# Attention's operands in a one-core hybrid SSD and attention block: queries stored as they are used, keys read with a doubled source, blank columns dropped

## The chip, the cores and the metric

One core of one Trainium2 chip. The metric is the device time of one execution in microseconds. All numbers below are of this kernel, which runs one whole layer in one program: projections, SSD scan, attention, merge, routed experts, output norm.

## The reference, cut to what matters

The layer has SEQ = 1024 latent and CTX = 256 context tokens, D_MODEL = 1024, 16 query heads and 4 key and value heads of 64. One input projection gives, among others, q, k and v. Latent q and k are rotated. A block of 128 latent queries reads all 256 context keys and the latent keys of three blocks, its own and its neighbours:

```python
kp = jnp.pad(k, ((0, 0), (WINDOW, WINDOW), (0, 0), (0, 0)))
vp = jnp.pad(v, ((0, 0), (WINDOW, WINDOW), (0, 0), (0, 0)))
def block(i):
    start = i * ATTN_BLOCK
    qb = lax.dynamic_slice_in_dim(qg, start, ATTN_BLOCK, axis=1)
    kb = lax.dynamic_slice_in_dim(kp, start, span, axis=1)
    ...
    s_loc = jnp.where(valid, s_loc, -jnp.inf)
    s_ctx = jnp.einsum("bqkrd,bskd->bkrqs", qb, k_ctx).astype(jnp.float32)
    p = jax.nn.softmax(jnp.concatenate([s_loc, s_ctx, s_sink], -1), axis=-1).astype(v.dtype)
```

The padded columns are masked. The output of the whole block is (1, 1024, 1024) in float32. Context queries aren't needed, as only the latent stream is put out.

## The kernel before, in words

The program is a row of stages, each one block in which every engine has its own list of instructions; engines order themselves by semaphores, and a stage's engines leave its block together. Float32 products are made of split operands: a number is kept as a high part `hi`, rounded to the type that TensorE multiplies, and the rest `lo`.

**Stage f** (`project_f_stage`) makes the outputs that have channels on partitions: x/B/C, then queries and keys (`NQK` = 10 tiles of 128 channels: 8 of queries with two heads each, 2 of keys), then gates. A tile of queries or keys is rotated, split by ScalarE (`keep_hi`, L575) and VectorE (`keep_lo`, L651) into the double-buffered tiles `qk_hi` and `qk_lo`, and stored by GpSimd (`store_split`, L710) to the DRAM tensors `qkH` and `qkL`. These have one row per channel and `KV_TOK` = 1536 columns: context, 128 blank columns, latent tokens, 128 blank columns. GpSimd fills the key rows' blanks with zeros at the stage's start (L695). ScalarE overwrites a buffer of `qk_hi` two tiles later, and waits for its store (`qk_out`, L574). After the tiles the same buffers take weights for another product.

**The states stage** stores the values token by token in `vT`, which has the same blanks (L1124, GpSimd); next GpSimd loads and scales chunks for the SSD states.

**The scan stage** (`scan_output_stage`) runs 32 units u: 8 chunks of 128 tokens times 4 groups. SyncE stores each unit's result `y` to `yT` (`store`, L1325), and behind the store it issues what `Early.load` (L1221) lists for this u: attention's first operands, into the slots of `shared` that the last chunks no longer need. Units 23, 24: the high keys, lower then upper 64 partitions. 25: query tile 0. 26: masks and identity. 27, 28: the low keys. 29: query tile 1. 30: another mask. `y` has one buffer per group, so the result of unit u is written (GpSimd's `finish`, L1533; the last unit's by VectorE, L1514) only when the store of unit u - 4 has landed. SyncE is one queue: what it issues late makes all behind it late.

**The attention stage** takes scores as two products in a row: a full one of 128 rows, `q` tile times `k1`, and one of 64 rows, times `k2` (L1674, L1678). The 128 rows of a query tile are the head's high part (64) and its low part (64), in this order for even heads and the other way round for odd ones; `k1` has the high keys twice, one copy in each half of the partitions, and `k2` the low keys twice. A query tile is 128 partitions x 16 heads x 128 queries. `load_query` (L1213) gathers it by four transfers, one for each half of the partitions and each parity of head; there are four buffers, and from tile 4 on SyncE loads tile m when tile m - 4 is scored. `load_key` (L1210) loads one half of the partitions for all four groups. Before its first score TensorE waits for both keys, the constants, and GpSimd's memset `a_ones` (L1846); VectorE waits for the sink (L1649, `a_negsink` L1807) and for all of `yT`'s stores, and each maximum (L1775) lets the next scores into the two score banks.

Of the kernel before, what the change touches and what calls it, by code (L numbers as in the profile page):

```python
# [23 lines left out]
P = 128  # L24
# [39 lines left out]
BLANK = WINDOW  # L64
KV_LAT0 = CTX + BLANK
KV_TOK = KV_LAT0 + SEQ + BLANK


def shape_constants():
# [13 lines left out]
    for b in range(LCHUNK):  # L83
# [3 lines left out]
    edges = np.stack([masks[:, :, CTX:CTX + P].transpose(0, 2, 1), masks[:, :, CTX + 2 * P:].transpose(0, 2, 1)], 2)  # L87
# [3 lines left out]
        "edges": np.ascontiguousarray(edges).reshape(LCHUNK, P, 2 * P),  # L91
# [5 lines left out]
        "flat": np.stack([np.zeros(KVH * KV_TOK, np.float32), np.ones(KVH * KV_TOK, np.float32)]),  # L97
# [225 lines left out]
def project_f_stage(s, cond_cols, mod, hi, lo, first, ahead, xbcF, xbcT, qkH, qkL, gF):  # L323
# [7 lines left out]
    with ExitStack() as st:  # L331
# [9 lines left out]
        zeros = own(st, nc, "f_zeros", [P, BLANK])  # L341
# [29 lines left out]
        zeros_made, blanks_out = s.sem("f_zeros_made"), s.sem("f_blanks_out")  # L371
# [18 lines left out]
        with nc.Block() as block:  # L390
# [297 lines left out]
            def _(pool):  # L688
                s.credit(pool, turned_out)

                pool.memset(zeros[:], 0.0).then_inc(zeros_made, 1)
                pool.wait_ge(zeros_made, 1)
                for part in (qkH, qkL):
                    for a in (CTX, KV_LAT0 + SEQ):
                        pool.dma_start(part[QH * HD:, a:a + BLANK].rearrange("(f p) t -> p f t", p=P),  # L695
                                       zeros[:].unsqueeze(1).to_broadcast([P, NQK - NQ, BLANK])).then_inc(blanks_out, 16)

# [39 lines left out]
                for b in range(2):  # L737
                    pool.wait_ge(qk_out[b], 16 * (NQK + NQK - NQ))
                    pool.wait_ge(turned_out[b], 8 * NT + 16)
# [7 lines left out]
                pool.wait_ge(blanks_out, 64)  # L747
                for b in range(2):
                    pool.wait_ge(qk_out[b], 16 * (NQK + NQK - NQ))
                    pool.wait_ge(wide_out[b], 8 * (NX - NXS))  # L750
                    pool.wait_ge(turned_out[b], 8 * NT + 16)
# [23 lines left out]
def project_states_stage(s, hi, lo, ahead, zT, vT, xbcT, tabs, cumrow, logrow, before):  # L775
# [20 lines left out]
    with ExitStack() as st:  # L796
# [4 lines left out]
        zeros = own(st, nc, "t_zeros", [P, VW])  # L801
# [25 lines left out]
        zeros_made, zeros_out = s.sem("t_zeros_made"), s.sem("t_zeros_out")  # L827
# [30 lines left out]
        with nc.Block() as block:  # L858

            @block.sync  # L860
            def _(sp):
# [5 lines left out]
                def store_v(n):  # L867
                    sp.wait_ge(acc_free, n + 1)
                    at = n * P if n < CCHUNK else KV_LAT0 + (n - CCHUNK) * P
# [237 lines left out]
            def _(pool):  # L1107
# [27 lines left out]
                pool.wait_ge(zeros_out, 32)  # L1135
# [43 lines left out]
class Early:  # L1179


    def __init__(self, s, st):
# [3 lines left out]
        NK, NQ, END = KVH * KV_TOK, QH * P, KVH * KV_TOK + QH * P  # L1186
# [34 lines left out]
    def load(self, s, eng, qkH, qkL, u):  # L1221
        low, high = slice(0, HD), slice(HD, P)
# [20 lines left out]
def scan_output_stage(s, later, early, qkH, qkL, xbcT, xbcF, zT, tabs, cumrow, logrow, before, yT):  # L1243
# [14 lines left out]
    with ExitStack() as st:  # L1258
# [39 lines left out]
        with nc.Block() as block:  # L1298

            @block.sync  # L1300
            def _(sp):
# [34 lines left out]
                for u in range(UNITS):  # L1336
                    store(u)
                    early.load(s, sp, qkH, qkL, u)
# [218 lines left out]
def attention_stage(s, later, early, yT, qkH, qkL, vT, aF):  # L1557
# [11 lines left out]
    NV = KV_TOK // P  # L1569
    STEP_COUNT = PAIRS + 4  # L1570

    def tiles(n):
        first = 1 if n == 0 else 0
        last = 2 if n == LCHUNK - 1 else 3
        return [(P * t, t) for t in range(CCHUNK)] + [(CTX + P * (t - first), CCHUNK + n + t) for t in range(first, last)]
# [1455 lines left out]
```

## Time and profile before

| what | before |
|---|---|
| runs | 2635.36, 2635.18, 2631.15 us; median 2635.18 |
| profiled execution, own time | 2638.86 us |
| its span, first to last instruction | 2637.1 us |
| TensorE busy | 2404.6 us, 91% |
| VectorE, ScalarE, GpSimd busy | 1696.2, 1140.2, 497.9 us |
| mean granted TensorE clock | 0.946 of full speed |
| DMA | 564.42 MB in 348009 packets, mean 214 GB/s |

A row of the profile names the line of the kernel, the engine, the operation, and `out<-in` by the program's names. A name with a q (SPq, POOLq) is an engine's sequencer: it issues DMAs and waits, and isn't counted as busy. "DMA share" is the mean busy share of the core's 16 DMA engines, and GB/s what they moved. "To landing" is the time from an issue to the last byte. Idle time of an engine that isn't the bottleneck costs nothing.

### The profile page before, as it was taken

How to read it: one execution, taken by the hardware profiler on the slowest of the kernel's cores; microseconds unless marked ns; L12 is line 12 of the kernel's file. 1: busy time of each engine (PE TensorE's matmuls, PEld its weight loads, DVE VectorE, ACT ScalarE, POOL GpSimd, SP SyncE). 2: the span in 40 equal slices, each digit the busy share in tenths (PEclk: the TensorE clock that was granted, in tenths of full speed). 3: DMA queues.
4: the chain of work that ended last, by engine and by line, in shares of the span. 5: the costliest groups of instructions: out<-in, count | busy, mean ns of one | idle time of the engine just before them, and what ended most of it. 6: DMA issues, size and time to landing. Idle time of an engine off the chain costs nothing. (4 is left out here: it accounts for less than half of the span.)

```text
span 2637.1 us, 34496 instructions
## 1 busy us (share of the span) xinstructions
PE 2404.6 (91%) x13468; PEld 1967.1 (75%) x13468; DVE 1696.2 (64%) x1900; ACT 1140.2 (43%) x1538; POOL 497.9 (19%) x410
## 2 busy tenths in 40 slices
PE   7899999999999997996999899998872999999992
PEld 2788888887798876664666599997762788888882
DVE  5555555544235663775666677665556899999996
ACT  3333332221123111454666644433332677777772
POOL 0000000011003440785111100001323011011112
PEclk9899999999999998988999999998975999999996
DMA  6222234776436875989331299895326899999994
GB/s 224 78 72 80 82 108 122 183 228 224 139 119 210 295 272 161 315 280 237 56 82 41 74 271 259 243 254 176 124 84 248 308 405 403 402 398 396 396 369 143
DMA packets 348009, 564.42 MB, mean 214 GB/s; under 512 B 22069, under 2 KB 257605, under 8 KB 325017
## 3 DMA queue, kind: packets, MB, share of 16 engines
q1 hardware_dynamic: 322522, 460.39, 52.3%
q0 software_dynamic: 23376, 97.36, 11.5%
q10 hardware_dynamic: 1968, 4.72, 0.5%
q8 instruction: 95, 1.56, 0.3%
q14 instruction: 48, 0.39, 0.0%
HBM read 452.74 MB, written 104.42 MB: 211 GB/s over the span
## 5 line engine op out<-in xcount | busy, mean ns | idle before, releaser
L2650 DVE TENSOR_TENSOR e_wlo<-e_w,e_whi 128x2048 fp32r<-128x2048 f32 x188 | 425.7, 2290 | 42.9 <-ACT e_whi L2599 41.6
L2599 ACT CAST e_whi<-e_w 128x2048 fp32r<-128x2048 f32 x192 | 365.4, 1910 | 124.7 <-PE e_gu L2776 83.5
L460 PE MATMUL f_lat<-h_hi,w_hi 128*128 128x512 f32 x800 | 253.9, 398 | 8.0 <-DVE w_lo L611 8.0
L460 PE MATMUL f_lat<-h_lo,w_hi 128*128 128x512 f32 x800 | 251.3, 395 | 0.0
L460 PE MATMUL f_lat<-h_hi,w_lo 128*128 128x512 f32 x800 | 251.1, 395 | 0.0
L2110 PE MATMUL b_acc<-b_hi,b_whi 128*128 128x256 f32 x768 | 218.7, 285 | 7.7 <-issue 7.7
L2110 PE MATMUL b_acc<-b_lo,b_whi 128*128 128x256 f32 x768 | 218.1, 284 | 0.0
L2110 PE MATMUL b_acc<-b_hi,b_wlo 128*128 128x256 f32 x768 | 218.1, 284 | 0.0
L611 DVE TENSOR_TENSOR w_lo<-w_raw,w_hi 128x1024 fp32r<-128x1024 f32 x50 | 61.2, 1226 | 171.6 <-ACT w_hi L530 171.6
L460 PEld LDWEIGHTS f_lat<-h_hi,w_hi 128*128 128x128 f32 x800 | 137.9, 189 | 38.3 <-DVE w_lo L611 8.6
L460 PEld LDWEIGHTS f_lat<-h_lo,w_hi 128*128 128x128 f32 x800 | 140.1, 188 | 29.9
L460 PEld LDWEIGHTS f_lat<-h_hi,w_lo 128*128 128x128 f32 x800 | 140.0, 188 | 29.8
L2110 PEld LDWEIGHTS b_acc<-b_hi,b_whi 128*128 128x128 f32 x768 | 148.3, 193 | 8.1 <-issue 8.1
L2110 PEld LDWEIGHTS b_acc<-b_lo,b_whi 128*128 128x128 f32 x768 | 148.2, 193 | 0.0
L2110 PEld LDWEIGHTS b_acc<-b_hi,b_wlo 128*128 128x128 f32 x768 | 148.2, 193 | 0.0
L625 DVE SCALAR_TENSOR_TENSOR conv_acc<-conv_in,conv_tap_cols,conv_acc 128x1284 f32<-128x1284 f32 (+1 forms) x96 | 145.0, 1511 | 3.4
L2776 PE MATMUL e_gu<-e_whi,e_xhi 128*128 128x512 f32 x512 | 140.3, 396 | 3.7 <-DVE e_xlo L2654 2.4
L2776 PE MATMUL e_gu<-e_wlo,e_xhi 128*128 128x512 f32 x512 | 138.7, 393 | 0.0
L2776 PE MATMUL e_gu<-e_whi,e_xlo 128*128 128x512 f32 x512 | 138.0, 392 | 0.0
L2845 POOL DMA_INDIRECT moe<-e_y,e_token x15 | 42.2, 2811 | 498.3 <-DVE e_y L2671 468.0
L1775 DVE CUSTOM_DVE_ANT_0 a_rows<-a_a_ps,shared 128x640 f32<-128x640 f32 (+1 forms) x128 | 96.0, 788 | 48.2 <-PE a_a_ps L1678 47.6
L1729 ACT ACTIVATE a_rows<-a_rows,a_negtop 128x640 f32<-128x640 f32 (+1 forms) x128 | 101.6, 796 | 31.1 <-DVE a_negtop L1781 31.0
(373 smaller groups left out, 5355.4 us busy)
## 6 DMA issues: line engine op xcount, KB each, us to landing
e_w<-in_w_gate_up SPq DMA_DIRECT2D x128, 1024.0 KB, 10.8
e_w<-in_w_down SPq DMA_DIRECT2D x64, 1024.0 KB, 9.0
w_raw<-in_w_in SPq DMA_DIRECT2D x50, 512.0 KB, 3.9
t_space<-xbcT POOLq DMA_DIRECT2D x18, 1280.0 KB, 6.2
before<-t_space SPq DMA_DIRECT2D x16, 1024.0 KB, 4.1
shared<-before SPq DMA_DIRECT2D x64, 256.0 KB, 6.4
l_w<-in_w_ssd_br SPq DMA_DIRECT2D x20, 768.0 KB, 6.9
xbcT<-t_out POOLq DMA_DIRECT2D x20, 640.0 KB, 4.4
```

Of the source, the lines that this page charges most:

```text
L460: mm = nc.tensor.matmul(o, weights[:, b, k, :], part[:, k, a:a + n], start=(k == 0 and n_pass == 0), stop=(k == KT - 1 and n_pass == 2))
L611: nc.vector.tensor_tensor(wlo[:, b], w[:, b], whi[:, b].bitcast(F32), ALU.subtract).then_inc(w_free, 1)
L625: nc.vector.scalar_tensor_tensor(conv[:, b, a:W_OUT], padded[:, b, a + c:c + W_OUT], tap[:, b, c:c + 1], conv[:, b, a:W_OUT], ALU.mult, AL ...
L1729: nc.scalar.activation(rows[:, h % RB, 0:w], rows[:, h % RB, 0:w], ACT.Exp, scale=SCALE, bias=negtop[:, h:h + 1], accum_out=sums[:, h:h + ...
L1775: V.tensor_tensor_reduce(rows[:, h % RB, 0:w], a_ps[:, h % 2, A0:A0 + w], mask[variant(n)][:, 0:w], 1.0, NEG, ALU.add, ALU.max, top[:, h:h ...
L2110: mm = nc.tensor.matmul(acc[:, b, int(k >= KY), 0:NW], weights[:, b, k, :], part[:, k, at:at + NW], start=(k in (0, KY) and n_pass == 0), ...
L2599: nc.scalar.copy(whi[:, slot % SPLIT], w[:, slot]).then_inc(w_hi, 1)
L2650: V.tensor_tensor(wlo[:, slot % SPLIT], w[:, slot], whi[:, slot % SPLIT].bitcast(F32), ALU.subtract).then_inc(w_split, 1)
L2776: mm = nc.tensor.matmul(gu[:, 512 * c:512 * c + 512], part[:, b, k, :], weights[:, slot % SPLIT, 512 * c:512 * c + 512], start=(k == 0 and ...
L2845: pool.indirect_dma_start(moe, bass.IndirectOffsetOnAxis(ap=token[:, e:e + 1], axis=0), y[:, e % 2], None, compute_op=ALU.add).then_inc(y_ ...
```

## The change

1. Queries go to a DRAM tensor `qS` that has 128 rows a head, laid out as a query tile needs them: the high part goes to blocks 0 and 3 of each pair of heads' four 64-row blocks (`heads[0::3]`), the low part to blocks 1 and 2. A query tile is then loaded by one transfer.
2. Keys go to `kH` and `kL` of 256 rows and `TOK` = 1280 columns. A load takes one group for all 128 partitions, from a source of shape [2, 64, 1280] that names the same 64 rows twice (step 0): four transfers a part, all four at unit 23 (high) and all four at unit 27 (low).
3. The blank columns of keys and values, their zeros and their stores are gone; column numbers in the attention follow. Two constants that nothing read are gone too.

```diff
 @@ project_f_stage, GpSimd
-                pool.memset(zeros[:], 0.0).then_inc(zeros_made, 1)
-                pool.wait_ge(zeros_made, 1)
-                for part in (qkH, qkL):
-                    for a in (CTX, KV_LAT0 + SEQ):
-                        pool.dma_start(part[QH * HD:, a:a + BLANK].rearrange("(f p) t -> p f t", p=P),
-                                       zeros[:].unsqueeze(1).to_broadcast([P, NQK - NQ, BLANK])).then_inc(blanks_out, 16)
...
                 def store_split(n):
-                    b, rows = n % 2, slice(n * P, n * P + P)
+                    b = n % 2
                     pool.wait_ge(qk_lo_made, n + 1)
-                    for part, kept in ((qkH, qhi), (qkL, qlo)):
-                        pool.dma_start(part[rows, KV_LAT0:KV_LAT0 + SEQ], kept[:, b, CTX:TOK].bitcast(F32)).then_inc(qk_out[b], 16)
-                        if n >= NQ:
-                            pool.dma_start(part[rows, 0:CTX], kept[:, b, 0:CTX].bitcast(F32)).then_inc(qk_out[b], 16)
+                    if n < NQ:
+                        heads = qS[2 * n * P:2 * n * P + 2 * P].rearrange("(x d) t -> x d t", d=HD)
+                        pool.dma_start(heads[0::3], qhi[:, b, CTX:TOK].bitcast(F32)).then_inc(qk_out[b], 16)
+                        pool.dma_start(heads[1:3], qlo[:, b, CTX:TOK].bitcast(F32)).then_inc(qk_out[b], 16)
+                    else:
+                        rows = slice((n - NQ) * P, (n - NQ) * P + P)
+                        pool.dma_start(kH[rows], qhi[:, b, 0:TOK].bitcast(F32)).then_inc(qk_out[b], 16)
+                        pool.dma_start(kL[rows], qlo[:, b, 0:TOK].bitcast(F32)).then_inc(qk_out[b], 16)
 @@ project_states_stage, GpSimd
-                pool.memset(zeros[:], 0.0).then_inc(zeros_made, 1)
-                pool.wait_ge(zeros_made, 1)
-                for at in (CTX, KV_LAT0 + SEQ):
-                    pool.dma_start(vT[at:at + BLANK, :], zeros[:]).then_inc(zeros_out, 16)
                 load_chunk(0)
 @@ Early
-    def load_key(self, eng, part, rows, out, sem):
-        eng.dma_start(out[rows].bitcast(F32), part[QH * HD:, :].rearrange("(g d) t -> d g t", d=HD)).then_inc(sem, 16)
-
-    def load_query(self, eng, qkH, qkL, m):
-        at, j = KV_LAT0 + m * P, m % len(self.q)
-        for half in range(2):
-            for odd in range(2):
-                part = qkH if half == odd else qkL
-                src = part[0:QH * HD, :].rearrange("(h o d) t -> o d h t", o=2, d=HD)[odd, :, :, at:at + P]
-                eng.dma_start(self.q[j][half * HD:half * HD + HD, odd::2].bitcast(F32), src).then_inc(self.q_in[j], 16)
+    def load_key(self, eng, part, out, sem):
+        for g in range(KVH):
+            eng.dma_start(out[:, g].bitcast(F32), part[g * HD:g * HD + HD, :].unsqueeze(0).to_broadcast([2, HD, TOK])).then_inc(sem, 16)
+
+    def load_query(self, eng, qS, m):
+        eng.dma_start(self.q[m % len(self.q)].bitcast(F32), qS.rearrange("(h p) t -> p h t", p=P)[:, :, m * P:m * P + P]).then_inc(self.q_in[m % len(self.q)], 16)
...
         if u == 23:
-            self.load_key(eng, qkH, low, self.k1, self.keys_in)
-        if u == 24:
-            self.load_key(eng, qkH, high, self.k1, self.keys_in)
+            self.load_key(eng, kH, self.k1, self.keys_in)
         if u == 25:
-            self.load_query(eng, qkH, qkL, 0)
+            self.load_query(eng, qS, 0)
...
         if u == 27:
-            self.load_key(eng, qkL, low, self.k2, self.keys_in)
-        if u == 28:
-            self.load_key(eng, qkL, high, self.k2, self.keys_in)
+            self.load_key(eng, kL, self.k2, self.keys_in)
         if u == 29:
-            self.load_query(eng, qkH, qkL, 1)
+            self.load_query(eng, qS, 1)
 @@ attention_stage, TensorE
-                        pe.wait_ge(q_in[n % len(q)], 64 * (n // len(q)) + 64)
-                    a, w = CTX + n * P + (P if n == 0 else 0), width(n) - CTX
+                        pe.wait_ge(q_in[n % len(q)], 16 * (n // len(q)) + 16)
+                    a, w = CTX + max(n - 1, 0) * P, width(n) - CTX
...
-                pe.wait_ge(keys_in, 64)
+                pe.wait_ge(keys_in, 32 * KVH)
```

Where SyncE's issues move: the end of the scan stage, from the last `y` stores ahead of the keys to the first attention loads. A row is the line, the transfer, and the shape of its destination (partitions first). Before:

```order
L1332 DMA yT<-l_wo 128x512 x4
L1211 DMA shared<-qkH 64x4x1536
L1332 DMA yT<-l_wo 128x512
L1211 DMA shared<-qkH 64x4x1536
L1332 DMA yT<-l_wo 128x512
L1219 DMA shared<-qkH 64x8x128
L1219 DMA shared<-qkL 64x8x128 x2
L1219 DMA shared<-qkH 64x8x128
L1332 DMA yT<-l_wo 128x512
```

Of the change (L1304 is the store of `y`, L1193 `load_key`, L1196 `load_query`):

```order
L1304 DMA yT<-l_wo 128x512 x4
L1193 DMA shared<-kH 128x1x1280 x4
L1304 DMA yT<-l_wo 128x512 x2
L1196 DMA shared<-qS 128x16x128
L1304 DMA yT<-l_wo 128x512
L1204 DMA shared<-const_masks 128x256
L1205 DMA shared<-const_masks 128x256
L1206 DMA shared<-const_squares 128x128
L1304 DMA yT<-l_wo 128x512
L1193 DMA shared<-kL 128x1x1280 x4
L1304 DMA yT<-l_wo 128x512 x2
```

The keys' upper half, which was issued behind unit 24's store, now goes out ahead of it with the rest, and each query tile is one row instead of four.

On GpSimd in stage f, where it stores the query tiles, before:

```order
L714 DMA qkH<-qk_hi 128x1024
L714 DMA qkL<-qk_lo 128x1024
L714 DMA qkH<-qk_hi 128x1024
L714 DMA qkL<-qk_lo 128x1024
L714 DMA qkH<-qk_hi 128x1024
```

and of the change:

```order
L700 DMA qS<-qk_hi 2x64x1024
L701 DMA qS<-qk_lo 128x1024
L700 DMA qS<-qk_hi 2x64x1024
L701 DMA qS<-qk_lo 128x1024
L700 DMA qS<-qk_hi 2x64x1024
```

The order is the same; the high part's destination is now two blocks of 64 rows apart from each other, the low part's two blocks lie together and stay one of 128.

## Rows read from the trace of the kernel before

**Rows 1.** The page: busy times of the engines, and the chain that ended last.

```profile
PE 2404.6 (91%) x13468; PEld 1967.1 (75%) x13468; DVE 1696.2 (64%) x1900; ACT 1140.2 (43%) x1538; POOL 497.9 (19%) x410
...
PE 21%; DVE 2%; DMA 1%; issue 0%; ACT 0%; POOLq 0%; DVEq 0%; ACTq 0%
```

**Rows 2.** Waits, 1185 to 1400 us: total us, times, longest.

```profile
PE a_a_ps L1674 <- POOL a_ones L1846: 13.1, 1, 13.1
```

**Rows 3.** Timeline, 1190 to 1242 us: start, duration, engine, line, operation, wait before.

```profile
1190.62 0.62 SPq L1211 DMA_DIRECT2D shared<-qkH  x1
...
1211.86 0.36 SPq L1332 DMA_DIRECT2D yT<-l_wo  x1
...
1221.79 7.59 SPq L1219 DMA_DIRECT2D shared<-qkL  x2
...
1226.58 0.69 DVE L1514 TENSOR_TENSOR l_wo<-l_w,l_wo 128x512 f32<-128x512 f32 x1
...
1230.78 3.75 SPq L1332 DMA_DIRECT2D yT<-l_wo  x1
...
1235.12 0.38 SPq L1332 DMA_DIRECT2D yT<-l_wo  x1
1235.89 0.33 SPq L1649 DMA_DIRECT2D a_sink<-in_attn_sink  x1
...
1241.83 0.18 DVE L1807 TENSOR_SCALAR a_negsink<-a_sink 128x16 f32<-128x16 f32 x1 [14.56 <-DMA a_sink<-in_attn_sink]
```

**Rows 4.** Busy time by stretch; last columns: granted clock, DMA share, GB/s.

```profile
core 0: us, PE busy (x) PEld busy (x) DVE busy (x) ACT busy (x) POOL busy (x), PEclk, DMA share, GB/s
455.00:565.00 110.00, 110.00 (x498) 89.72 (x497) 54.20 (x47) 28.72 (x30) 12.71 (x24) 1.00 0.71 188
...
736.00:780.00 44.00, 44.00 (x319) 44.00 (x318) 9.52 (x8) 14.36 (x30) 1.78 (x4) 1.00 0.37 128
...
1190.00:1236.00 46.00, 32.66 (x170) 22.62 (x168) 28.58 (x46) 19.15 (x70) 34.10 (x30) 0.91 1.03 226
...
1232.00:1236.00 4.00, 0.00 (x0) 0.00 (x0) 0.00 (x0) 0.00 (x0) 0.09 (x1) 0.50 1.17 225
...
1262.00:1300.00 38.00, 37.16 (x267) 24.33 (x266) 24.56 (x68) 24.28 (x57) 4.08 (x4) 1.00 0.22 43
...
2100.00:2300.00 200.00, 200.00 (x928) 166.54 (x927) 185.16 (x98) 148.38 (x88) 24.49 (x12) 1.00 1.01 397
```

**Rows 5.** DMA issues: count, KB each, median us to landing.

```profile
shared<-qkH SPq DMA_DIRECT2D x2, 1536.0 KB, 12.4
...
squares<-const_squares SPq DMA_DIRECT2D x1, 64.0 KB, 1.8
```

**Rows 6.** DMA queues (packets, MB, share), and ACT's issues.

```profile
q10 hardware_dynamic: 1968, 4.72, 0.5%
...
e_w<-moe ACTq DMA_DIRECT2D x8, 256.0 KB, 6.1
...
out<-e_w ACTq DMA_DIRECT2D x3, 512.0 KB, 2.6
...
y_all_cum<-cumrow ACTq DMA_DIRECT2D x64, 8.0 KB
...
y_all_cum<-const_lanes ACTq DMA_DIRECT2D x4, 128.0 KB
```

**Rows 7.** The tile `qk_hi`: count, durations in ns, first and last start.

```profile
L575 ACT CAST qk_hi<-f_out x10: 1047/1050/1272, 450.7 to 557.0; 128x1024 fp32r<-128x1024 f32 x8, 128x1280 fp32r<-128x1280 f32 x2
...
L714 POOL DMA_DIRECT2D qkH<-qk_hi x10: 532/532/534, 455.4 to 560.1; - x10
```

**Rows 8.** The blanks: GpSimd's timeline from 735 us.

```profile
735.85 0.31 POOL L1121 MEMSET t_zeros<- 128x256 f32 x1 [57.08 <-DMA gF<-conv_in]
...
737.54 0.54 POOL L1112 DMA_DIRECT2D t_space<-xbcT  x1
```

More of the change, by code:

```diff
@@ L320, in _, with project_f_stage @@
                     split(n)
-def project_f_stage(s, cond_cols, mod, hi, lo, first, ahead, xbcF, xbcT, qkH, qkL, gF):
+def project_f_stage(s, cond_cols, mod, hi, lo, first, ahead, xbcF, xbcT, qS, kH, kL, gF):
     nc = s.nc
@@ L340, in project_f_stage @@
         wide = own(st, nc, "f_out", [P, 2, TOK])
-        zeros = own(st, nc, "f_zeros", [P, BLANK])
         turned = own(st, nc, "t_out", [P, 2, TOK])
@@ L737, in _ @@
                 for b in range(2):
-                    pool.wait_ge(qk_out[b], 16 * (NQK + NQK - NQ))
+                    pool.wait_ge(qk_out[b], 16 * NQK)
                     pool.wait_ge(turned_out[b], 8 * NT + 16)
@@ L800, in project_states_stage @@
         rows = own(st, nc, "t_rows", [P, STAGED, VW])
-        zeros = own(st, nc, "t_zeros", [P, VW])
         tab = own(st, nc, "t_tab", [P, NCHUNK, 5, W])
@@ L868, in store_v @@
                     sp.wait_ge(acc_free, n + 1)
-                    at = n * P if n < CCHUNK else KV_LAT0 + (n - CCHUNK) * P
+                    at = n * P
                     sp.dma_start(vT[at:at + P, :], rows[:, n % STAGED]).then_inc(rows_out[n % STAGED], 16)
@@ L1185, in __init__ @@
         one, two, three = (SLOT * j for j in range(3))
-        NK, NQ, END = KVH * KV_TOK, QH * P, KVH * KV_TOK + QH * P
+        NK, NQ, END = KVH * TOK, QH * P, KVH * TOK + QH * P
         KEYS = CTX + 3 * P
@@ L1208, in slot, with load @@
         return x, bc, before, cum
[L1210 to L1222 removed]
+    def load_key(self, eng, part, out, sem):
[3 more added lines that the diff above has]
+        eng.dma_start(self.q[m % len(self.q)].bitcast(F32), qS.rearrange("(h p) t -> p h t", p=P)[:, :, m * P:m * P + P]).then_inc(self.q_in[m % len(self.q)], 16)
+    def load(self, s, eng, qS, kH, kL, u):
         if u == 23:
[L1224 to L1226 removed]
+            self.load_key(eng, kH, self.k1, self.keys_in)
         if u == 25:
[L1228 removed]
+            self.load_query(eng, qS, 0)
         if u == 26:
@@ L1233, in load, with scan_output_stage @@
         if u == 27:
-            self.load_key(eng, qkL, low, self.k2, self.keys_in)
-        if u == 28:
-            self.load_key(eng, qkL, high, self.k2, self.keys_in)
+            self.load_key(eng, kL, self.k2, self.keys_in)
         if u == 29:
-            self.load_query(eng, qkH, qkL, 1)
+            self.load_query(eng, qS, 1)
         if u == 30:
             eng.dma_start(self.mask[1], s.masks[1]).then_inc(self.mask_in, 16)
-def scan_output_stage(s, later, early, qkH, qkL, xbcT, xbcF, zT, tabs, cumrow, logrow, before, yT):
+def scan_output_stage(s, later, early, qS, kH, kL, xbcT, xbcF, zT, tabs, cumrow, logrow, before, yT):
     nc = s.nc
@@ L1337, in _ @@
                     store(u)
-                    early.load(s, sp, qkH, qkL, u)
+                    early.load(s, sp, qS, kH, kL, u)
                     if u % G == G - 1 and u // G + NB < LCHUNK:
@@ L1554, in _, with attention_stage @@
                         finish(u)
-def attention_stage(s, later, early, yT, qkH, qkL, vT, aF):
+def attention_stage(s, later, early, yT, qS, kH, kL, vT, aF):
     nc = s.nc
@@ L1568, in attention_stage @@
     RB, TB, VB = 10, 3, 8
-    NV = KV_TOK // P
+    NV = TOK // P
     STEP_COUNT = PAIRS + 4
@@ L1574, in tiles @@
         last = 2 if n == LCHUNK - 1 else 3
-        return [(P * t, t) for t in range(CCHUNK)] + [(CTX + P * (t - first), CCHUNK + n + t) for t in range(first, last)]
+        return [(P * t, t) for t in range(CCHUNK)] + [(CTX + P * (t - first), CCHUNK + n - 1 + t) for t in range(first, last)]
     def width(n):
@@ L1600, in attention_stage @@
         sink, negsink = own(st, nc, "a_sink", [P, QH]), own(st, nc, "a_negsink", [P, QH])
-        v = own(st, nc, "a_v", [P, NV - 2, KVH * HD])
+        v = own(st, nc, "a_v", [P, NV, KVH * HD])
         top, negtop, sums, sunk, inverse = (own(st, nc, f"a_{n}", [P, LCHUNK * QH]) for n in ("top", "negtop", "sums", "sunk", "inverse"))
@@ L1650, in _ @@
                 sp.dma_start(v[:, 0:CCHUNK], vT[0:CTX, :].rearrange("(c p) n -> p c n", p=P)).then_inc(v_in, 16)
-                sp.dma_start(v[:, CCHUNK:], vT[KV_LAT0:KV_LAT0 + SEQ, :].rearrange("(c p) n -> p c n", p=P)).then_inc(v_in, 16)
-                early.load_query(sp, qkH, qkL, 2)
-                early.load_query(sp, qkH, qkL, 3)
+                sp.dma_start(v[:, CCHUNK:], vT[CTX:TOK, :].rearrange("(c p) n -> p c n", p=P)).then_inc(v_in, 16)
+                early.load_query(sp, qS, 2)
+                early.load_query(sp, qS, 3)
                 sp.dma_start(mask[2], s.masks[LCHUNK - 1]).then_inc(last_mask, 16)
@@ L1659, in _ @@
                         sp.wait_ge(scored, QH * (m - len(q) + 1))
-                        early.load_query(sp, qkH, qkL, m)
+                        early.load_query(sp, qS, m)
             @block.tensor
@@ L2963, in program @@
         s = Stage(nc, inputs, out, ctx)
-        s.squares, s.cosine, s.sine, s.masks, s.edges, s.lanes, s.flat = (constants[n] for n in ("squares", "cosine", "sine", "masks", "edges", "lanes", "flat"))
+        s.squares, s.cosine, s.sine, s.masks, s.lanes = (constants[n] for n in ("squares", "cosine", "sine", "masks", "lanes"))
         cond_cols, mod = s.scratch("cond_cols", [P, KT]), s.scratch("mod", [1, 6 * D])
         xbcF, xbcT = s.scratch("xbcF", [CONV_CH, TOK]), s.scratch("xbcT", [TOK, CONV_CH])
-        qkH, qkL = s.scratch("qkH", [(QH + KVH) * HD, KV_TOK]), s.scratch("qkL", [(QH + KVH) * HD, KV_TOK])
+        qS, kH, kL = s.scratch("qS", [2 * QH * HD, SEQ]), s.scratch("kH", [KVH * HD, TOK]), s.scratch("kL", [KVH * HD, TOK])
         gF = s.scratch("gF", [2 * D, SEQ])
-        zT, vT = s.scratch("zT", [SEQ, D_INNER]), s.scratch("vT", [KV_TOK, KVH * HD])
+        zT, vT = s.scratch("zT", [SEQ, D_INNER]), s.scratch("vT", [TOK, KVH * HD])
         tabs, cumrow = s.scratch("tabs", [NCHUNK, P, 5 * 2 * HEADS]), s.scratch("cumrow", [LCHUNK, 2, 2 * HEADS, P])
@@ L2981, in program @@
             ahead = Ahead(s, st)
-            project_f_stage(s, cond_cols, mod, hi, lo, first, ahead, xbcF, xbcT, qkH, qkL, gF)
+            project_f_stage(s, cond_cols, mod, hi, lo, first, ahead, xbcF, xbcT, qS, kH, kL, gF)
             project_states_stage(s, hi, lo, ahead, zT, vT, xbcT, tabs, cumrow, logrow, before)
@@ L2990, in program @@
                     early = Early(s, shared)
-                    scan_output_stage(s, later, early, qkH, qkL, xbcT, xbcF, zT, tabs, cumrow, logrow, before, yT)
-                    attention_stage(s, later, early, yT, qkH, qkL, vT, aF)
+                    scan_output_stage(s, later, early, qS, kH, kL, xbcT, xbcF, zT, tabs, cumrow, logrow, before, yT)
+                    attention_stage(s, later, early, yT, qS, kH, kL, vT, aF)
                 branch_stage(s, later, yT, aF, gF, mF)
```

13 lines of the change are left out of this document (1 added, 12 removed).

## The prediction

> **What bounds the kernel now.** I read the page first: TensorE is busy 91% of the span, and the chain that ended last is TensorE work [rows 1]. A change that issues no matmul differently can pay or cost only where TensorE is short of data. So I looked for such a place near the queries and keys. The waits of the stretch 1185 to 1400 us show one: the first attention scores (L1674) wait 13.1 us, in a single piece, and are let go by `a_ones` (L1846) [rows 2]. That memset is no work to speak of; it is the first thing GpSimd does in the attention stage, so what ended there is the scan stage's block, and every engine leaves it together.
>
> The timeline shows which engine was last. VectorE finished its last unit at 1226.58 + 0.69 = 1227.27 us, but SyncE issued the store of that unit only at 1235.12 [rows 3]. SyncE was held by its own issues: the second and third of four pieces of query tile 1 took 7.59 us together, the store behind them 3.75, against 0.33 to 0.62 for an issue that is not held. The queue was full: over 1190 to 1236 us the 16 DMA engines were busy at a share of 1.03, yet moved only 226 GB/s, while the experts' loads at a share of 1.01 move 397 GB/s [rows 4]. In that stretch the keys go out as rows of 64 partitions at a time (the text of the change and the order rows show the shapes), in the experts all 128. After the block SyncE issues the load of the sink; it lands when VectorE's `a_negsink` can start, at 1241.83, and the first softmax work follows. From 1262 us on attention is not held by transfers: DMA share 0.22, TensorE 37.2 of 38 us busy [rows 4].
>
> **The change, part by part.** *Query loads.* Four transfers of 64 partitions and 256 KB become one of 128 partitions and 1024 KB. By the two rates a tile takes 1.049 MB / 226 GB/s = 4.6 us now and 1.049 / 397 = 2.6 us then. Only tiles 0 and 1 stand ahead of the attention's start.
>
> *Key loads.* Each of two key parts was two transfers of 1536 KB [rows 5]; now it is four of 128 x 1280 elements, 0.655 MB each, eight in all, 5.24 MB instead of 6.29. Their source is `part[...].unsqueeze(0).to_broadcast([2, HD, TOK])`: its outermost dimension has 2 entries, where the one that it replaces had 64. What does an outermost 2 do here? The page's queue rows tell: all ACT's loads and stores go through q10, 1968 packets [rows 6]. Of these, the three `out` stores and eight `moe` loads have 128 rows, and close the count at 128 + 16 packets each, 1584; the four loads of `const_lanes` have 16 rows, 16 + 16 each, 128. That leaves 1968 - 1584 - 128 = 256 for the 64 loads of `cumrow`, 4 each: 2 rows of 4 KB and 2 completions, not 16. A transfer with 2 rows is thus run by two DMA engines. [...]
>
> The rate of one engine is 397 / 16 = 24.8 GB/s [rows 4]. One key transfer on two: 0.655 MB / 49.6 GB/s = 13.2 us. I take the same two engines for all eight, since they are issued on one queue in the same form: 8 x 13.2 = **105.7 us** of serial work, against 6.29 MB / 226 GB/s = 28 us now. The first is issued at 1190.62 us as before [rows 3], since nothing on SyncE ahead of it changed; the first data moves about 1.5 us later (a 64 KB transfer lands in 1.8 in all [rows 5]). The other transfers put a sixteenth on each engine, and stand in line on these two: four `yT` stores of 256 KB, 4 x 0.66 us; query tile 0, 2.6; masks and identity, 0.4. So the last key row lands at 1190.6 + 1.5 + 105.7 + 2.6 + 2.6 + 0.4 = **1303.4 us**. SyncE's last issue of the block comes at about 1304, since the queue holds only so much: it was held 7.59 us over two issues with one key transfer and a few hundred query rows ahead of them [rows 3]. Against 1235.50 that is +68.5. Behind it the sink's load took 5.9 us, with query tile 1 before it in the queue; with that tile in 2.6 instead of 4.6 us it is some 2 us quicker. **Sum: +67 us.**
>
> *Who else waits.* The stores of units 24 to 27 stand behind the first key part on the two engines and land from about 1245 on. GpSimd's `finish` of unit u waits for the store of u - 4, so units 28 to 31 move from 1219 to 1227 us to some 1245 to 1262. That is still before 1303, and costs nothing more. Unit 27 waits for no store issued behind the keys, so the second key part is issued without a gap.
>
> *Query stores (stage f).* The high halves now go as 2 x 64 rows (the order rows), so by the same reasoning on two engines: 0.524 MB / 49.6 = 10.6 us. ScalarE overwrites that buffer two tiles later: ten casts between 450.7 and 557.0 us, so 23.6 us per two tiles, less the 4.7 from the cast to the store's issue at 455.4 [rows 7]. 10.6 fits in 18.9, and TensorE is busy 110 of 110 us there [rows 4]. I take 0; with the weights' loads sharing these engines the bound is +5. The stores' own number falls by a few; nobody waits for them.
>
> *Blanks gone.* Six transfers and two memsets: four of `f_zeros` early in stage f, and two of `t_zeros` at 736 us [rows 8]. GpSimd idled 57 us before the latter, and its next load is issued 1.7 us earlier, with TensorE busy 44 of 44 us around it [rows 4, 8]. 0. Keys, values and masks have the same widths as before in every matmul: 0.
>
> [...]
>
> The profiled execution took 2638.86 us, so I expect 2706 there; the median of three runs, 2635.18, lies 3.7 below it, so **2702 us**. About 0.2% (5 us) is what a measurement of this kernel can tell from no change.
>
> [...]
>
> **Rivals.** *B, 16 engines serve each key load (destination decides).* Keys and queries all run at 397 GB/s. SyncE is then idle when unit 31 is ready at 1227.3, issues its store there and not at 1235.12, and the sink lands sooner, as little is queued: -7.7 to -11 us, **2626 us**. For it: 128 partitions do run twice as fast as 64 in rows 4. Against: the count of rows 6. It decides if the engine count comes from the written side. 8%.
>
> *C, two engines each, but another pair for each load.* Four at once take 13.2 us: the second part, issued behind unit 27's store at 1211.86 and in about 2.5 us, lands near 1229, so attention starts some 6 us earlier than now: **2629 us**. Against: nothing in the rows shows an engine's number, for or against. 3%.
>
> *D, two engines, each at the rate of the 64-partition loads*, 226 / 16 = 14.1 GB/s, for instance because both copies read the same source rows. 5.24 MB / 28.2 = 186 us, 80 more than in the sum: **2782 us**. Against: those loads shared whatever halves their rate among 16 engines, two would not. 5%.
>
> **How the numbers follow.** My forecast has 84%. Its own range: an engine nearly alone may run some 10% above 24.8 GB/s, and the stores and query may hide in it (-10, -6): 2685. ACT's loads on the same two engines, short query rows of 512 bytes (a share above 1 moving little, rows 4), the query stores' +5 and a delayed last unit give up to +25: 2727. The range 2684 to 2727 leaves out B, C, D, and little of A. Chances: faster 0.10 (B, C), same 0.01, slower 0.89.
>
> **What the profile would show.** Right: landings of the eight key loads that climb in steps of about 13 us to over 40; a DMA share near 2/16 and some 50 GB/s between 1245 and 1300 us; one wait of L1674 of about 80 us ending near 1304; `l_wo` (L1546) of units 28 to 31 waiting for the `yT` store; nothing new in stage f; attention's own rows as before, only later. Wrong: key landings under 10 us and an earlier start (B or C); steps of 23 us (D); a new DMA wait of `w_hi` or `qk_hi` in stage f, which would say that the query stores weren't free.

## The result, and the profile after

| | kernel before | changed kernel |
|---|---|---|
| median, us | 2635.27 (2631.15 to 2638.38, 4 runs) | **2715.1** (2710.88 to 2717.56, 4 runs) |
| ratio, 95% interval | | **1.0296** [1.0281, 1.031] |
| profiled execution, us (span) | 2638.86 (2637.1) | 2710.88 (2709.2) |

The change costs 80 us between the medians and 72 between the two profiled executions: the profile of before is a slow one (2638.86 us, above each of the four), that of after is the fastest of its four. The forecast was 2702, range 2684 to 2727. This section accounts for the 72 us of the profiles; the 8 us between them and the medians are taken up by the experiments.

The page of the changed kernel:

```profile
PE 2407.1 (89%) x13468; PEld 1969.8 (73%) x13468; DVE 1697.0 (63%) x1900; ACT 1141.0 (42%) x1538; POOL 493.5 (18%) x398
...
q10 hardware_dynamic: 1968, 4.72, 0.5%
```

TensorE does the same work as in [rows 1], 2407 against 2405 us; only its share fell. The time is idle time. The waits of 1185 to 1400 us say where (total us, times, longest):

```profile
PE a_a_ps L1646 <- POOL a_ones L1817: 54.4, 1, 54.4
DVE a_negsink L1778 <- DMA a_sink<-in_attn_sink: 52.9, 1, 52.9
...
POOL l_wo L1518 <- DMA yT<-l_wo: 33.0, 1, 33.0
```

The first is the wait of [rows 2], there 13.1. The third is new: GpSimd's `finish` of a late scan unit waits 33 us for the `y` store four units earlier. Which queue holds that store is seen in SyncE's issues, 1185 to 1345 us (start, duration, line, transfer; a store or key load that is not held is issued in 0.3 to 0.6 us, a query tile in 1.5):

```profile
1191.61 25.98 SPq L1193 DMA_DIRECT2D shared<-kH  x4
1217.71 13.61 SPq L1304 DMA_DIRECT2D yT<-l_wo  x2
1231.37 1.52 SPq L1196 DMA_DIRECT2D shared<-qS  x1
1233.00 15.63 SPq L1304 DMA_DIRECT2D yT<-l_wo  x1
...
1250.59 24.94 SPq L1193 DMA_DIRECT2D shared<-kL  x4
1275.64 14.68 SPq L1304 DMA_DIRECT2D yT<-l_wo  x2
1290.37 1.53 SPq L1196 DMA_DIRECT2D shared<-qS  x1
1292.01 15.69 SPq L1304 DMA_DIRECT2D yT<-l_wo  x1
...
1308.28 0.39 SPq L1304 DMA_DIRECT2D yT<-l_wo  x1
1309.07 0.33 SPq L1621 DMA_DIRECT2D a_sink<-in_attn_sink  x1
```

In [rows 3] the last store stood at 1235.12 and the sink at 1235.89: both are 73.2 us later. The rhythm is that of one key transfer. Four key loads are issued in 25 to 26 us, and the tile view shows how that is spread (min/median/max, ns):

```profile
L1193 SPq DMA_DIRECT2D shared<-kH x4: 544/6183/12929, 1191.6 to 1204.7; - x4
L1193 SPq DMA_DIRECT2D shared<-kL x4: 499/5986/12337, 1250.6 to 1263.2; - x4
```

Two of the four are hardly held. The third and the fourth are held 11.4 to 12.9 us each, and the stores behind them 13 to 14. So SyncE got no more than about two such transfers ahead. Busy time by stretch gives the rate (columns as in [rows 4]); the two of 6 and 30 us are stretches in which almost nothing but keys moves:

```profile
455.00:565.00 110.00, 108.94 (x492) 88.79 (x491) 53.88 (x47) 29.27 (x30) 12.46 (x19) 1.00 0.66 176
...
1240.00:1246.00 6.00, 0.00 (x0) 0.00 (x0) 0.00 (x0) 0.00 (x0) 0.00 (x0) 0.50 0.13 52
...
1256.00:1286.00 30.00, 0.00 (x0) 0.00 (x0) 4.54 (x4) 0.00 (x0) 3.86 (x3) 0.50 0.13 52
...
1245.00:1300.00 55.00, 3.64 (x16) 3.49 (x16) 6.33 (x6) 1.74 (x8) 11.37 (x9) 0.50 0.28 88
```

A share of 0.13 is two engines of 16, and 52 GB/s is 26 each: at that rate 0.655 MB takes 12.6 us. The packets agree: from 1256 to 1286 us, 305 of 5120 bytes start, 0.200 us each, 2.03 at work at a time. From 1245 to 1300 us TensorE works 3.6 of 55 us at a granted clock of 0.50, and the DMA engines move 88 GB/s, where [rows 4] had 226 in the corresponding place. Attention's own work is unchanged: 237.4 us of TensorE in 244 us, clock 0.98, both from 1244.4 us in the kernel before and from 1316 in this one. The last row to read is in the first line above: TensorE, 110 of 110 us in [rows 4], now misses 1 us in stage f. The waits of 400 to 600 us name it, one of DMA that was not there:

```profile
ACT qk_hi L567 <- DMA qS<-qk_lo: 12.5, 2, 7.9
```

and the landings of stage f's query stores (median us, last column) have 17.5 us, where the kernel before had 6.2:

```profile
qS<-qk_hi POOLq DMA_DIRECT2D x8, 512.0 KB, 4.9
qS<-qk_lo POOLq DMA_DIRECT2D x8, 512.0 KB, 17.5
```

High and low store add to one semaphore, so I read the 17.5 at the second as the landing of the later of the two; e4 bears that out, where only the high store is changed and this number falls to 6.6.

### The profile page after: what moved, and what is told of

Its sections match the earlier page's. It is cut to its first block and busy times, and to the rows that moved or that the text cites. A ratio compares the mean times of both kernels' runs of the same rounds, so it can differ in the third digit from the quotient of the medians.

```text
span 2709.2 us, 34462 instructions
## 1 busy us (share of the span) xinstructions
PE 2407.1 (89%) x13468; PEld 1969.8 (73%) x13468; DVE 1697.0 (63%) x1900; ACT 1141.0 (42%) x1538; POOL 493.5 (18%) x398
## 3 DMA queue, kind: packets, MB, share of 16 engines
q10 hardware_dynamic: 1968, 4.72, 0.5%
```

## The experiments

**How they are read.** All kernels issue the same 13,468 matmuls in the same order, so the start of matmul number n can be set against that of the kernel before. Two differences are used throughout, in each kernel's profiled execution: how much it falls behind *in stage f* (from the matmul that started at 427 us before to that at 729) and *at the boundary* from scan to attention (from 1219.06 to 1248).

| kernel | stage f | boundary | median, us | ratio to before, interval |
|---|---|---|---|---|
| the change | +1.3 | +70.7 | 2715.1 | 1.0296 [1.0281, 1.031] |
| e1 | +5.2 | -8.2 | 2632.17 | 0.9985 [0.9976, 0.9994] |
| e2 | 0.0 | +94.6 | 2729.77 | 1.0345 [1.0327, 1.0363] |
| e3 | +7.3 | -10.0 | 2640.18 | 1.0013 [1.0003, 1.0022] |
| e4 | +2.0 | -9.1 | 2631.96 | 0.9983 [0.9975, 0.9992] |
| e5 | +7.7 | +72.0 | 2720.67 | 1.0325 [1.0295, 1.0355] |
| e6 | +8.8 | +25.8 | 2672.84 | 1.0143 [1.0102, 1.0184] |
| e7 | +2.4 | +68.8 | 2709.35 | 1.0282 [1.025, 1.0313] |
| e8 | +2.1 | +37.9 | 2678.07 | 1.0163 [1.0132, 1.0194] |
| e9 | 0.0 | -8.0 | 2627.91 | 0.997 [0.9959, 0.9982] |
| e10 | 0.0 | +70.9 | 2707.7 | 1.0273 [1.0257, 1.0289] |
| e11 (the change again) | +5.7 | +70.4 | 2712.82 | 1.0296 [1.0282, 1.031] |
| e12 (e10 again) | 0.0 | +70.8 | 2706.26 | 1.0274 [1.0259, 1.0289] |

**e1, only the shape of the key loads taken back.** Theory: the outermost 2 puts each load on two engines. Rival: something else in the change (the new query layout, the issue of all keys at unit 23) costs the 70 us.

```diff
-        for g in range(KVH):
-            eng.dma_start(out[:, g]..., part[g * HD:g * HD + HD, :].unsqueeze(0).to_broadcast([2, HD, TOK]))
+        for half in range(2):
+            eng.dma_start(out[half * HD:half * HD + HD]..., part.rearrange("(g d) t -> d g t", d=HD))
```

> The changed kernel, but each key part is loaded by two transfers of 64 partitions x 4 groups x 1280 (leading dimension 64 on both sides), both at unit 23 (high) and unit 27 (low). Theory (a leading 2 in the source leaves two DMA engines for a load): all 16 engines serve the keys again, 5.24 MB at the 226 GB/s of 64-partition loads, 23 us; SyncE's last issue of the scan stage falls to about 1231 us, and the time to about 2631 us (2625 to 2637), within 10 us of the kernel before. Rival 1 (the loss comes from the queries: the new layout of qS, or a 1 MB load of 512-byte rows): it stays near 2700. Rival 2 (loading all of a key part at once, at unit 23, blocks the y stores): it stays well above 2650.

The rest of the change stays, and the 71 us are gone:

```profile
1193.79 1.30 SPq L1193 DMA_DIRECT2D shared<-kH  x2
```

1.30 us for the whole part, landing in 12.8. What remains of the change gains 8.2 us at the boundary: the sink is issued at 1232.14 us, against 1235.89 in [rows 3], although the kernel comes 3.2 us late to the boundary. But most of the gain had been lost in stage f (+5.2), where ScalarE's `qk_hi` waited 16.8 us for the query stores.

**e2, only the key loads changed**, in the kernel before (its 1536 columns, everything else as it was).

```diff
+        for g in range(KVH):
+            at = QH * HD + g * HD
+            eng.dma_start(out[:, g]..., part[at:at + HD, :].unsqueeze(0).to_broadcast([2, HD, KV_TOK]))
```

> The kernel before, with its queries, blanks and 1536 columns, and only the key loads of the change: four transfers a part from a source of [2, 64, 1536], at units 23 and 27. Theory: two engines, 64 rows of 6144 bytes each at 26 GB/s, 15.1 us a transfer, 121 us for eight; against the 100 us of the changed kernel 20 more, and the query tiles go at the old rate (4.6 instead of 2.6 us twice): about 2730 us (2715 to 2745). Rival 1 (the queries carry the loss): 2635. Rival 2 (the cost is one of each transfer, not of its bytes): as the changed kernel, 2715.

+94.6 us at the boundary by this edit alone. Four issues take 31.3 us, so one load holds SyncE about 15; 12.6 x 1536 / 1280 = 15.1. The cost goes by bytes on the two engines. Stage f, with the old query stores, loses nothing.

```profile
1189.31 31.32 SPq L1213 DMA_DIRECT2D shared<-qkH  x4
```

**e3, keys stored twice** in DRAM (eight 64-row stores a tile instead of two stores of 128 rows), loaded once a part by one plain 128-partition transfer.

```diff
-        for g in range(KVH):
-            eng.dma_start(out[:, g]..., part[g * HD:g * HD + HD, :].unsqueeze(0).to_broadcast([2, HD, TOK]))
+        eng.dma_start(out..., part.rearrange("(g p) t -> p g t", p=P))
```

> The changed kernel, but the keys are stored twice in DRAM (64-row stores, eight a tile of keys instead of two), 128 rows a group, so that one transfer of 128 partitions x 4 groups x 1280 loads a part. Theory: 16 engines at the 397 GB/s of 128-partition loads, 6.6 us a part; SyncE is free when unit 31 is ready at 1227 us, and the attention starts 8 to 11 us earlier than in the kernel before: 2626 us (2622 to 2632), with the query stores' 1.3 us in it. Rival (the 64-partition form was no slower, the stretch was bound by HBM or by bytes): no faster than the version with halves. More stores of keys in stage f: nobody waits for them; if the ada loads behind them do, +5 at most.

A miss. The boundary gains 10.0 us, the most of all, but stage f gives back 7.3, so that the kernel is no better than before. The waits of 400 to 620 us:

```profile
DVE conv_acc L664 <- DMA qk_hi<-in_w_ada: 19.8, 4, 17.0
...
ACT qk_hi L567 <- DMA qS<-qk_lo: 12.3, 2, 7.9
```

VectorE waits for the `w_ada` loads, which GpSimd issues behind the key stores; the longest such wait was 3.3 in the kernel before. e4 tells how much of this is the query stores.

**e4, e3 with the high query half in two 64-row stores**, so that no transfer of the kernel has an outermost 2.

```diff
-                        pool.dma_start(heads[0::3], qhi[:, b, CTX:TOK]...)
+                        pool.dma_start(heads[0], qhi[0:HD, b, CTX:TOK]...)
+                        pool.dma_start(heads[3], qhi[HD:P, b, CTX:TOK]...)
```

> As keys stored twice, and the high half of each query tile is stored by two transfers of 64 rows instead of one of 2 x 64. Theory: in the changed kernel ScalarE waited 12.5 us in all (two waits) in stage f for the store of qS, since two engines serve a 2 x 64 store; TensorE got 1.3 us late there. Both go: 1 to 2 us faster than keys stored twice, 2625 us, more than a measurement shows, so the trace decides (no wait of qk_hi for qS). Rival (the wait came from stores as such, not from their shape): three stores a tile make it longer.

8.2 us less than e3, with intervals that do not touch, where 1 to 2 was expected. ScalarE's wait for `qS` is gone and the stores land in 6.6 us instead of 17.8. This was the first number to say that the two-engine query stores are not free.

**e5 and e6, no broadcast at all: what does the outermost dimension do by itself?** The keys stand in DRAM as 2 blocks of 64 rows, or 4 of 32, with one unused row between blocks so that they can't be merged; the bytes of a load are the same.

```diff
+        blocks = part.rearrange("(g b r) t -> g b r t", b=2, r=65)
-            eng.dma_start(out[:, g]..., part[g * HD:g * HD + HD, :].unsqueeze(0).to_broadcast([2, HD, TOK]))
+            eng.dma_start(out[:, g]..., blocks[g][:, 0:64, :])
```

(e6: `b=4, r=33` and `0:32`.)

> The changed kernel, keys stored twice in DRAM as 2 blocks of 64 rows a group with one unused row between blocks, and loaded group by group from a source of [2, 64, 1280] whose two copies lie apart (no step of 0). Theory (the count of the leading dimension decides, not the step of 0): as the changed kernel, 12.5 us a transfer, about 2712 us (2700 to 2725). Rival (reading the same rows twice is what is slow): near 2630.

> The same with 4 blocks of 32 rows a group: source [4, 32, 1280], destination 128 partitions. Theory: four engines, 6.3 us a transfer, 50 us for the eight keys loads instead of 100. The queue's end then falls by about 50 us: some 2660 us (2650 to 2675). Rival (any source that isn't one row list of 128 goes to two engines, or one pair): 2712. Rival (16 engines): 2630.

```profile
1199.31 27.03 SPq L1197 DMA_DIRECT2D shared<-kH  x4
```

```profile
1201.54 9.41 SPq L1197 DMA_DIRECT2D shared<-kH  x4
```

With 2 blocks the boundary costs 72.0 us, as with the broadcast (70.7): reading the same rows twice is not what costs. With 4 blocks it costs 25.8. The packets of 5120 bytes, which only the key loads have at this place, pass in e6's trace in 31.7 and 30.9 us for the two parts, in that of the change in 53.6 and 52.2. That is 43.2 us less, and 70.7 - 43.2 = 27.5, near the 25.8. Both lose 7.7 and 8.8 us in stage f, with e3's many key stores and the change's query stores; so they are read by the boundary.

**e7, the second key part issued by ScalarE.** Does another queue find other engines?

```diff
-        if u == 27:
-            self.load_key(eng, kL, self.k2, self.keys_in)
@@ scan stage, ScalarE
+                    if u == 29:
+                        act.wait_ge(y_made, 28)
+                        early.load_key(act, kL, early.k2, early.keys_low)
```

> The changed kernel, but the four loads of the low keys are issued by ScalarE (its own queue) after its work on unit 29, once unit 27's y is made. Theory (a load with a leading 2 goes to the same two engines from either queue): the two engines' work is the same, only the 7 us gap between the parts may go, and the held issue also holds ScalarE: 2700 to 2720 us. Rival (the limit is SyncE's queue, or the pair is another for each queue): the low keys load beside the high ones, attention starts some 40 to 50 us earlier, near 2665.

```profile
1192.22 28.84 SPq L1194 DMA_DIRECT2D shared<-kH  x4
...
1215.69 25.46 ACTq L1194 DMA_DIRECT2D shared<-kL  x1
...
1221.18 27.56 SPq L1303 DMA_DIRECT2D yT<-l_wo  x2
```

It does not. One issue on ScalarE's queue is held 25.5 us, twice the 12.6, while SyncE's stores behind the first part are held 27.6. From 1222 to 1240 us key rows of both queues pass, 5.0 a microsecond on SyncE's and 5.2 on ScalarE's, and the DMA share is still 0.13 and the rate 52 GB/s: the two queues share the same two engines and each gets half. The total shift at attention is that of the change (+70.4 against +71.7 at the matmul of 1248), and ScalarE now stands in line as well.

**e8, the second part issued by GpSimd**, behind unit 27.

> The same, with the four low loads issued by GpSimd after its work on unit 27. Theory of two fixed engines for every issuer: as with ScalarE, 2700 to 2720. [...]

```profile
1196.00:1209.00 13.00, 12.77 (x72) 9.43 (x72) 10.35 (x23) 6.74 (x27) 11.88 (x11) 1.00 0.13 54
1216.00:1227.00 11.00, 3.88 (x21) 2.43 (x19) 1.82 (x2) 2.26 (x9) 0.54 (x1) 0.85 0.51 181
1230.00:1240.00 10.00, 0.00 (x0) 0.00 (x0) 0.00 (x0) 0.00 (x0) 0.00 (x0) 0.50 0.13 52
```

```profile
1189.23 30.59 SPq L1194 DMA_DIRECT2D shared<-kH  x4
...
1244.78 16.25 SPq L1303 DMA_DIRECT2D yT<-l_wo  x1
...
1274.18 0.33 SPq L1623 DMA_DIRECT2D a_sink<-in_attn_sink  x1
```

GpSimd issues its four loads at 1209.6 to 1212.8 us. SyncE's keys alone keep two engines busy (share 0.13). With GpSimd's loads beside them it is about eight (share 0.51, 181 GB/s). So GpSimd's transfers go to different engines, and rival C is right for GpSimd's queue while it is wrong for SyncE's and ScalarE's. One of the four still meets SyncE's pair: SyncE's 5120-byte packets, which pass at 10.2 a microsecond in the change's stretches of keys alone, pass at 4.8 from 1216 to 1240 us. From 1230 to 1240, GpSimd's pass beside them at 5.0, and both together make the 52 GB/s of the third line. SyncE's first key part takes from 1190.6 to 1259.1 us, 68.5 instead of 53.6.

The profile's median landing of these four loads, 10.4 us, is not the time of one load, since the four count on one semaphore. The last of its 64 increments comes at 1263.8 us, although the last key row was read at 1240. What was still moving on GpSimd's queue in between were 4-byte packets. Besides the 512 key packets it carries 3648 of them, 912 for each load, where a load of the same shape on SyncE's queue has 2 (below). 2860 of the 3648 pass by 1215.3 us, 396 from 1227.1 to 1229.8, and the other 392 from 1240.8 to 1263.4, beside SyncE's last key packets and behind them. So here the four loads were complete only with the last 4-byte packets, 23 us behind the last key row. My estimate of what they are rests on the counts alone: 912 = 14 x 64 + 16, or 64 for each engine that carries none of the load's rows, and 16 increments. Three loads on other pairs would then have 3 x (2 x 64 + 2) = 390 of them waiting on SyncE's pair, near the 392.

The boundary costs 37.9 us against the change's 70.7, and the median is 2678.07 us, below the 2700 to 2720 of two fixed engines for every issuer. What is left is SyncE's own key part, which holds its queue: attention's `a_sink` goes out at 1274.18.

Which of the 16 engines are SyncE's pair, no run here shows.

**e9, e1 and e4's query stores together**: the change without any transfer of two engines.

> The changed kernel with each key part loaded by two 64-partition transfers whose leading dimension is 64 (as in e1) and the high half of the queries stored by two 64-row stores (as in e4). If the two-engine spread of the query stores costs stage f what e1 and e4 lost and regained there, PE's waits on a query tile for an earlier query store are gone, the store lands in 6 to 8 us instead of 17, and the time is e1's 2632 less 3 to 8 us: 2624 to 2629. If that loss came from something else (the units behind it, the clock), 2632 again.

2627.91 us, within the 2624 to 2629 expected, 0.3% below the kernel before. Nothing is lost in stage f, and the boundary keeps its 8.0.

**e10, the change with only the query stores mended**; then **e11**, the change itself once more, and **e12**, e10 once more, on one chip beside each other.

> The changed kernel as it is, keys read twice on two engines, with only the high half of the queries stored by two 64-row stores. If the query stores cost stage f what e3 and e4 differ by (8.2 us), 2705 to 2709. If they cost only the 1.3 us by which the profile of the changed kernel falls back there, 2710 to 2714. If nothing (the prediction's zero), 2715. The stretch at the start of attention should still grow by 70 to 71 us in all three.

> The changed kernel unaltered, a second profiled execution and more times, beside e12 on the same chip. Its first profiled execution fell back by only 1.3 us in stage f, yet the one edit to the query stores was worth some 7 us between medians. If the two-engine query stores cost a varying amount, this execution should lose another amount there (3 to 9 us), and the medians of e11 and e12 should lie 5 to 9 us apart. If the 7 us were a difference between chips, the medians lie within 3 us.

> The kernel of e10 (changed kernel, high query half stored by two 64-row stores) once more. 5 to 9 us below e11 if the query stores' two engines cost that; within 3 us if they don't. Stage f should again fall back by nothing.

e12 is 6.6 us below e11; e10 lies 7.4 below the first runs of the change. Stage f falls back by nothing in e10 and e12, but by 1.3 in one profiled execution of the change and by 5.7 in the other. So the cost of the query stores varies from execution to execution, and the first profile caught a cheap one. In the whole table, kernels with the two-engine query stores lose 1.3 to 8.8 us in stage f, those without 0.0 to 2.0. In e11 it can be followed from start to end; ScalarE's timeline, then VectorE's and TensorE's (in brackets the wait before, and for what):

```profile
508.10 1.01 ACT L554 COPY f_out<-f_lat 128x1024 f32<-128x1024 f32 x1 [3.88 <-PE f_lat L452]
519.18 1.04 ACT L567 CAST qk_hi<-f_out 128x1024 fp32r<-128x1024 f32 x1 [10.07 <-DMA qS<-qk_lo]
520.13 1.04 ACT L522 CAST w_hi<-w_raw 128x1024 fp32r<-128x1024 f32 x1
...
521.20 1.22 DVE L603 TENSOR_TENSOR w_lo<-w_raw,w_hi 128x1024 fp32r<-128x1024 f32 x1 [6.28 <-ACT w_hi L522]
...
522.48 0.73 PE L452 MATMUL f_lat<-h_hi,w_hi 128*128 128x512 f32 x2 [3.22 <-DVE w_lo L603]
```

`keep_hi` waits 10 us for a query store, the next weights' `w_hi` stands behind it on ScalarE, `w_lo` on VectorE behind that, and TensorE runs dry for 3.2 us. The granted clock is lower as well, 0.68 over 522 to 526 us, where it was 1.00 in the kernel before: another 4 x 0.32 = 1.3 us. Together 4.5 of the 5 us by which the matmuls slip at this place.

The query stores come with 4-byte packets, too: on GpSimd's queue 12165 packets pass from 400 to 600 us in the change and 5179 in e10, with nearly the same bytes (18.5 and 18.7 MB). Over the whole execution that queue has 10080 of 4 bytes in the change and 3040 in e10, 7040 = 8 x (912 - 2 x 16) more: 912 for each 2 x 64 store, as for each load of e8. They use next to none of the engines' time (that queue's share is 27.9% against 27.7%). Whether these stores are complete only with the last of them, as e8's loads were, or late by the rows that each of two engines has to move beside everything else, no run separates.

## Why the prediction was right, and its misses

**Right: the side that decides.** The sum prices a key load, with 2 on its source's side and 128 on its destination's, at two engines, and so a query store with 128 and 2. No row of before shows that; what [rows 6] gives is a load of 2 rows. The trace bears that reading out: of q10's 1968 packets, 1024 have 2048 bytes, 512 have 4096, 64 have 8192, and 368 have 4, which is 16 for each of the 11 transfers of 128 rows and the 4 of 16 rows, and 2 for each of the 64 with 2 rows. The same count answers the question for the keys. On SyncE's queue the change has 15141 packets of 4 bytes and e1 has 15189, 48 more: 4 x 16 against 8 x 2. With e5's 2 blocks there are 15141 again, with e6's 4 blocks 15157, 16 more, so 4 a load. The times go with the counts: e1 takes the 2 away and with it the 71 us; a part of 2.62 MB takes 53.6 and 52.2 us in the change, 55.2 and 53.3 with e5's 2 blocks and no broadcast, 31.7 and 30.9 with e6's 4. B (16 engines), at 8%, falls. C, at 3%, falls for this kernel, though e8's share of 0.51 shows it for GpSimd's queue. D (14.1 GB/s an engine) falls: 26 GB/s.

**Right: serial on one pair, and nothing else.** e2 has the whole cost by this one edit. TensorE's work, the blanks and the clock at the boundary add nothing that the profile shows: the granted clock is 0.50 in the idle stretch of both kernels (1232 to 1236 us before, 1245 to 1300 of the change) and 0.98 over attention's 244 us in both.

**The terms at the boundary**, predicted 67 and measured 71.7 (`a_negsink` at 1313.48 against 1241.83):

- The time of the keys was right. Their 5120-byte packets pass from 1193.4 to 1247.0 and from 1253.8 to 1306.0 us, 53.6 + 52.2 = 105.8 us against 105.7. Alone the pair would need 12.6 us a load; it loses the rest where `y` stores and a query tile pass beside the keys.
- The start is 1.0 us later than in the profile of before (1191.61 against 1190.62), and the first packet comes 1.8 us behind the issue instead of 1.5: +1.3.
- "The second key part is issued without a gap." This step failed. SyncE was held 15.63 us with the unit-26 store behind query tile 0, and issued the second part only at 1250.59, when the first had already been read; between the parts lie 6.8 us. That it costs no more than +1.2 is luck: the sum had put 5.6 us on the pair for the stores, the tile and the masks, and these now pass mostly inside the gap.
- So the last key row comes at 1306.0, not 1303.4. The last store was issued at 1308.28, 2.3 us behind it where 0.6 had been allowed (+1.7): the store before it was held 15.69 us with query tile 1 ahead of it in the queue. The sink came 1.5 us quicker, not 2 (+0.5).

Together these are +4.8 us, and +4.7 was measured.

**The size of the wait was wrong.** Expected: one wait of L1674 of about 80 us. It is 54.4, at L1646, ending 1309.5. The prediction let units 28 to 31 run at 1245 to 1262 itself, and then counted the wait as if TensorE had stopped at 1227. The end of a wait is what sets the time; its length depends on what was done in between. (The profile gives no landing for SyncE's key loads, so that their landings climb in steps of 13 us, the first sign named, couldn't be read; the held issues and the packets stand in its place.)

**The bandwidth of the stretch**, "some 50 GB/s", left out what the other 14 engines move: 4 x 0.655 MB of keys, a query tile of 1.05 and four `y` stores of 0.26 make 4.7 MB in 55 us, 86 GB/s, against 88 measured. In the stretches with keys alone it was 52, at 2/16.

**The query stores: taken as 0, bound +5, measured 6.6 to 7.4 us.** "10.6 fits in 18.9" failed, and of the steps that failed this one cost most. 10.6 us is what two engines would need alone, at the sum's 24.8 GB/s each; beside weights, `t_out` and `w_ada` on the same engines the stores land in a median of 17.5, and the two or three slower ones pass the margin. The text named the sign of it ("a new DMA wait of `qk_hi`"), and it was there. The 100% busy TensorE of [rows 4] was no cover either: ScalarE's queue, where `keep_hi` stands ahead of `w_hi`, carried the wait to it.

So 2702 + 4.7 at the boundary + 7 in stage f = 2714, and 2715.1 was measured.

**Where the expected gain is.** What the new layout gives (one 128-row transfer for a query tile, 128-row key stores, no blanks) is the -8 to -9 us of e1, e4 and e9; no run separates the three (e4 also stores and loads its keys in another form). It could only be seen with the two-engine transfers taken away. In the change it lies under 106 us of serial loads.

## What to carry to other kernels

A transfer of many rows is not yet a transfer on many engines: the key loads filled 128 partitions at a DMA share of 0.13. Read the outermost dimension of both access patterns as the instruction has it, after slicing, broadcasting or gaps. Here a key load led by a 2 took its bytes / 52 GB/s (rows of 5120 bytes), in line with all like it from SyncE and ScalarE (e7), and transfers of 64 partitions beat it (e1: -8.2 us at the boundary instead of +70.7). A store that "fits" alone must be given its landing beside the other traffic, and what waits for it followed through the queue of the engine that waits: here a late store reached TensorE in four steps.

## What the runs showed of the hardware

- **SyncE got about two such transfers ahead of its queue.** Each has 128 rows of 5120 bytes; from the third on every issue was held for about one transfer (11.4 to 12.9 us), and the stores behind them on SyncE too (13 to 14). With four blocks (e6) the four loads were issued in 9.4 us, in e1's form (two loads a part) in 1.3.
- **GpSimd's four loads at once worked on different engines, SyncE's and ScalarE's on the same two** (e8: a DMA share of 0.51 where SyncE alone has 0.13; e7: 25.5 us for one issue, when both queues use the pair).
- **The two-engine loads of GpSimd came with 4-byte packets, and were complete only with the last of them** (e8: 3648 for four loads, the last at 1263.4 and the last increment at 1263.8 us, 23 us behind the last key row).
- **More, smaller stores on GpSimd's queue went with later loads behind them**: with e3's eight key stores a tile instead of two, and twice the bytes, VectorE waited up to 17.0 us for `w_ada` (3.3 before); in e4, with nothing left on two engines, it still waits 15.6, though stage f then loses only 2.0 us. Which property of these stores does it was not tried.
- **The slip in stage f varies** for one and the same kernel, 1.3 and 5.7 us in two profiled executions. What makes it so is open.
